# FFN of a four-layer model on one core: the high weight tile takes the operand's high and low parts in one 512-column matmul, and the two halves of the bank are added at eviction

## The reference

```python
def swiglu(h, w_gate, w_up, w_down):
    return (jax.nn.silu(h @ w_gate) * (h @ w_up)) @ w_down
# in each layer
h = h + mixer(rms_norm(h, mixer_g))
h = h + swiglu(rms_norm(h, ffn_g), w_gate, w_up, w_down)
```

## Time and profile before

| | us |
|---|---|
| median of three runs | 1203.58 (1201.99 to 1203.69) |
| the profiled execution's own time | 1202.35 |
| its span, first to last instruction | 1200.5 |
| PE busy | 1177.2, 98% of the span |
| DVE busy | 811.6, 68% |
| ACT busy | 589.2, 49% |
| mean DMA rate | 165 GB/s |

### The profile page before, as it was taken

One profiled execution on the slowest core, in us unless ns is written; L12 is line 12 of the kernel. 1 busy time (PEld: TensorE's weight loads), 2 busy tenths in 40 slices (PEclk: granted clock), 3 DMA queues, 4 the chain that ended last, 5 costly groups with the idle time before them and its releaser, 6 DMA issues.

```text
span 1200.5 us, 22339 instructions
## 1 busy us (share of the span) xinstructions
PE 1177.2 (98%) x9228; PEld 1142.8 (95%) x9228; DVE 811.6 (68%) x1302; ACT 589.2 (49%) x965; POOL 30.7 (3%) x54
## 2 busy tenths in 40 slices
PE   8999999999999799999999999999999899999999
PEld 8999999999998699999999999999998569999999
DVE  6867766655899577666656967666554897766642
ACT  6535444444745464445543545444444566544531
POOL 0120000000000000000000000000001200000000
PEclk8999999999999799999999999999999999999999
DMA  7543555555222045555543645555553323555551
GB/s 293 211 141 140 176 176 181 193 189 176 106 106 71 28 184 180 188 192 182 180 169 142 222 170 195 186 176 178 209 176 141 140 72 140 177 180 191 192 181 66
DMA packets 29046, 197.91 MB, mean 165 GB/s; under 512 B 3472, under 2 KB 4752, under 8 KB 5520
## 3 DMA queue, kind: packets, MB, share of 16 engines
q1 hardware_dynamic: 28656, 196.34, 45.7%
q10 hardware_dynamic: 288, 0.14, 0.0%
HBM read 195.41 MB, written 1.05 MB: 164 GB/s over the span
## 4 chain that ended last, share of the span: by engine, by line
PE 96%; DVE 2%; ACT 1%; DMA 0%; issue 0%; POOL 0%; DVEq 0%; ACTq 0%
PE banks L353 28%; PE banks L356 28%; PE banks L359 28%; PE banks L390 7%; PE banks L373 1%; PE banks L379 1%; PE banks L376 1%; DMA col<-cols 0%; PE banks L1276 0%; DVE scr L1493 0%; POOL scr L900 0%; DVE lo_t L284 0%; DVE scr L1476 0%; ACT scr L1337 0%; DVE scr L1481 0%
## 5 line engine op out<-in xcount | busy, mean ns | idle before, releaser
L353 PE MATMUL banks<-xh,hi_t 128*128 128x256 f32 x1856 | 530.0, 286 | 2.2 <-ACT hi_t L278 2.2
L359 PE MATMUL banks<-xh,lo_t 128*128 128x256 f32 x1856 | 526.3, 284 | 0.5 <-DVE lo_t L284 0.5
L356 PE MATMUL banks<-xl,hi_t 128*128 128x256 f32 x1856 | 526.3, 284 | 0.0
L284 DVE TENSOR_TENSOR lo_t<-raw_t,hi_t 128x1024 fp32r<-128x1024 f32 x368 | 444.8, 1221 | 12.2 <-ACT hi_t L278 7.7
L278 ACT ACTIVATE hi_t<-raw_t 128x1024 fp32r<-128x1024 f32 x368 | 380.6, 1048 | 71.2 <-PE banks L359 48.3
L353 PEld LDWEIGHTS banks<-xh,hi_t 128*128 128x128 f32 x1856 | 357.3, 192 | 3.0 <-ACT hi_t L278 2.4
L359 PEld LDWEIGHTS banks<-xh,lo_t 128*128 128x128 f32 x1856 | 357.3, 192 | 0.8 <-DVE lo_t L284 0.8
L356 PEld LDWEIGHTS banks<-xl,hi_t 128*128 128x128 f32 x1856 | 357.3, 193 | 0.6 <-issue 0.2
L353 PE MATMUL banks<-fh,hi_t 128*128 128x256 f32 x960 | 274.8, 286 | 4.8 <-ACT fh L1000 3.3
L356 PE MATMUL banks<-fl,hi_t 128*128 128x256 f32 x960 | 272.7, 284 | 0.5 <-DVE fl L840 0.4
L359 PE MATMUL banks<-fh,lo_t 128*128 128x256 f32 x960 | 272.3, 284 | 0.0
(11 more groups left out here) (160 smaller groups left out, 660.8 us busy)
## 6 DMA issues: line engine op xcount, KB each, us to landing
raw_t<-w SPq DMA_DIRECT2D x183, 1024.0 KB, 4.8
raw_t<-w SPq DMA_DIRECT2D x2, 512.0 KB, 7.0
out<-h SPq DMA_DIRECT2D x8, 128.0 KB, 3.7
cst<-consts SPq DMA_DIRECT2D x1, 800.0 KB, 11.1
h<-xT SPq DMA_DIRECT2D x1, 768.0 KB, 7.3
h<-xT SPq DMA_DIRECT2D x1, 256.0 KB, 4.2
pw<-poolw SPq DMA_DIRECT2D x1, 256.0 KB, 13.1
col<-cols SPq DMA_DIRECT2D x1, 193.0 KB, 8.1
```

The lines of the kernel that those rows point to most:

```text
L284: e.tensor_tensor(lo_t[:, p % RING, :], raw_of(p), hi_t[:, p % RING, :].bitcast(F32), ALU.subtract).then_inc(s_lo, 1)
L353: e.matmul(dst, hi_t[:, slot, c], hi[:, k, :], start=first, stop=False, skip_group_check=True)
L356: e.matmul(dst, hi_t[:, slot, c], lo[:, k, :], start=False, stop=False, skip_group_check=True)
L359: m = e.matmul(dst, lo_t[:, slot, c], hi[:, k, :], start=False, stop=last, skip_group_check=True)
```

## The change

The operand's two parts lie side by side in one tensor (`x2`, `f2`), so that they are 512 contiguous columns. In the FFN alone, `broad_tile` takes the place of `tile`: one matmul of 512 columns with the high weight tile fills a whole bank (high by high in columns 0 to 255, high by low in 256 to 511), and one of 256 columns with the low weight tile accumulates into the first half. Both parts of the operand are waited for before the first matmul. A block `u` now fills two banks, a pair of `PAIRS`, of which there are three; the RMS work of the FFNs moves to bank 2. At eviction ACT copies the second halves of the pair to SBUF (`side`), DVE adds the first halves to it (`add`, which frees the pair), and the scaling then reads and writes SBUF. On ACT the split that was due after the silu stands before it. For a row of the second product DVE adds the two halves to `h` one after the other, the second after the first is complete. The mixers keep `tile`.

```diff
-        xh = sb("xh", [P, KD, T], F32R)
-        xl = sb("xl", [P, KD, T], F32R)
-        fh = sb("fh", [P, KF, T], F32R)
-        fl = sb("fl", [P, KF, T], F32R)
+        x2 = sb("x2", [P, KD, 2, T], F32R)
+        f2 = sb("f2", [P, KF, 2, T], F32R)
+        xh, xl, fh, fl = x2[:, :, 0, :], x2[:, :, 1, :], f2[:, :, 0, :], f2[:, :, 1, :]
...
+        def broad_tile(e, g, bank, k, parts, first, last, arrives=None):
+            slot, r = piece(e, g)
+            c = slice(r * P, (r + 1) * P)
+            if r == 0:
+                e.wait_ge(s_hi, g // 8 + 1)
+            if arrives:
+                e.wait_ge(*arrives[0])
+                e.wait_ge(*arrives[1])
+            e.matmul(halves(banks[:, bank, :]), hi_t[:, slot, c], parts[:, k, :, :], start=first, stop=False,
+                     skip_group_check=True)
+            if r == 0:
+                e.wait_ge(s_lo, g // 8 + 1)
+            m = e.matmul(banks[:, bank, 0:T], lo_t[:, slot, c], parts[:, k, 0, :], start=False, stop=last,
+                         skip_group_check=True)
+            if g in MARKS:
+                m.then_inc(s_tiles, 1)
...
         def dve_ffn(e, f):
+            def add(u):
+                e.wait_ge(s_side, KF * f + u + 1)
+                e.tensor_tensor(halves(t_ring[u % 3]), pair_of(u, 0), halves(b_ring[u % 2]), ALU.add).then_inc(s_up, 1)
             lo_to(e, g0 + 32)
             dve_mean(e, i)
+            add(0)
             dve_dg(e, i)
+            add(1)
...
             for u in range(KF):
                 lo_to(e, c)
-                e.wait_ge(s_tiles, upto(g0 + 16 * max(u, 1) + 15))
-                e.tensor_tensor(halves(t_ring[u % 3]), halves(banks[:, UP_BANKS[u % 4], :]), ..., ALU.mult).then_inc(s_up, 1)
+                if u >= WIDE:
+                    add(u)
+                both = halves(t_ring[u % 3])
+                e.wait_ge(s_up, KF * f + u + 1)
+                e.tensor_tensor(both, both, stretch(rbc[:, :], 1, 2), ALU.mult).then_inc(s_scaled, 1)
...
-                e.tensor_tensor(h[:, n, :], banks[:, DOWN_BANKS[n % 3], 0:T], h[:, n, :], ALU.add).then_inc(s_h, 1)
+                m = dv.mark(e.tensor_tensor(h[:, n, :], ps[:, 0:T], h[:, n, :], ALU.add))
+                e.wait_ge(dv.sem, m)
+                e.tensor_tensor(h[:, n, :], ps[:, T:2 * T], h[:, n, :], ALU.add).then_inc(s_h, 1)
...
         def act_ffn(e, f):
+            def side(u):
+                e.wait_ge(s_tiles, upto(g0 + 16 * max(u, 1) + 15))
+                if u >= 2:
+                    e.wait_ge(s_up, KF * f + u - 1)
+                e.activation(halves(b_ring[u % 2]), pair_of(u, 1), ACT.Copy).then_inc(s_side, 1)
+            hi_to(e, g0 + 32)
+            side(0)
+            side(1)
             for u in range(KF):
                 hi_to(e, c)
-                e.wait_ge(s_up, KF * f + u + 1)
+                if u >= WIDE:
+                    side(u)
+                hi_to(e, c + 3)
+                e.wait_ge(s_scaled, KF * f + u + 1)
                 if u >= 2:
                     e.wait_ge(s_gated, KF * f + u - 1)
                 e.activation(s_ring[u % 2], t_ring[u % 3][:, 0:T], ACT.Silu).then_inc(s_silu, 1)
-                hi_to(e, c + 3)
```

More of the change, by code:

```diff
@@ L134 @@
 UP_BANKS = (0, 1, 6, 2)
[L135 removed]
+PAIRS = (0, 6, 4)
+DOWN_BANKS = (3, 7, 6)
 OUT_BANKS = (2, 3, 4, 5)
@@ L138, with rms_bank @@
 RMS_BANK = 7
+def rms_bank(i):
+    return 2 if i % 2 else RMS_BANK
 def att_banks():
@@ L343, in piece, with tile @@
             return p % RING, r
-        def tile(e, g, dst, k, hi, lo, first, last, arrives=None):
+        def tile(e, g, dst, k, parts, first, last, arrives=None):
             slot, r = piece(e, g)
@@ L352, in tile @@
                 e.wait_ge(*arrives[0])
-            e.matmul(dst, hi_t[:, slot, c], hi[:, k, :], start=first, stop=False, skip_group_check=True)
+            e.matmul(dst, hi_t[:, slot, c], parts[:, k, 0, :], start=first, stop=False, skip_group_check=True)
             if arrives:
                 e.wait_ge(*arrives[1])
-            e.matmul(dst, hi_t[:, slot, c], lo[:, k, :], start=False, stop=False, skip_group_check=True)
+            e.matmul(dst, hi_t[:, slot, c], parts[:, k, 1, :], start=False, stop=False, skip_group_check=True)
             if r == 0:
                 e.wait_ge(s_lo, g // 8 + 1)
-            m = e.matmul(dst, lo_t[:, slot, c], hi[:, k, :], start=False, stop=last, skip_group_check=True)
+            m = e.matmul(dst, lo_t[:, slot, c], parts[:, k, 0, :], start=False, stop=last, skip_group_check=True)
+            if g in MARKS:
[14 more added lines that the diff above has]
+                         skip_group_check=True)
             if g in MARKS:
@@ L401, in dve_mean @@
             e.wait_ge(s_col_sums, i + 1)
-            m = e.tensor_scalar(st[:, 0, :], banks[:, RMS_BANK, 0:2], 1.0 / D, EPS, ALU.mult, ALU.add)
+            m = e.tensor_scalar(st[:, 0, :], banks[:, rms_bank(i), 0:2], 1.0 / D, EPS, ALU.mult, ALU.add)
             if i == 4:
-                m = e.tensor_scalar(st[:, 2, :], banks[:, RMS_BANK, 2:4], 1.0 / D, None, ALU.mult)
+                m = e.tensor_scalar(st[:, 2, :], banks[:, rms_bank(i), 2:4], 1.0 / D, None, ALU.mult)
             m.then_inc(s_mean, 1)
@@ L419, in pe_spread @@
             e.wait_ge(s_dg, DG_AT[i] + n)
-            plain(e, banks[:, RMS_BANK, 0:n * P], one[:, :],
+            plain(e, banks[:, rms_bank(i), 0:n * P], one[:, :],
                   dg4[:, 0:n, :].rearrange("p a b -> p (a b)")).then_inc(s_spread, 1)
@@ L424, in dve_rbc @@
             e.wait_ge(s_spread, RBC_AT[i] + 1)
-            e.tensor_copy(rbc[:, :], banks[:, RMS_BANK, 0:T]).then_inc(s_rbc, 1)
+            e.tensor_copy(rbc[:, :], banks[:, rms_bank(i), 0:T]).then_inc(s_rbc, 1)
             e.wait_ge(s_rbc, RBC_AT[i] + 1)
-        s_up, s_silu, s_gated = sem("up"), sem("silu"), sem("gated")
+        s_side, s_up, s_scaled, s_silu, s_gated = sem("side"), sem("up"), sem("scaled"), sem("silu"), sem("gated")
         t_ring = [scratch(n * 512, 512) for n in range(3)]
@@ L433, in model_kernel, with pair_of @@
         m_ring = [scratch(2048 + n * T, T) for n in range(2)]
+        b_ring = [scratch(2560 + n * 512, 512) for n in range(2)]
+        def pair_of(u, half):
+            return banks[:, PAIRS[u % 3]:PAIRS[u % 3] + 2, half * T:(half + 1) * T]
         def pe_ffn(e, f):
@@ L439, in pe_ffn @@
                     for t in range(2):
-                        tile(e, g0 + 4 * k + 2 * v + t, banks[:, UP_BANKS[v], t * T:(t + 1) * T], k, xh, xl,
-                             k == 0 and t == 0, k == KD - 1, x_of(i, k) if v == 0 and t == 0 else None)
+                        broad_tile(e, g0 + 4 * k + 2 * v + t, PAIRS[v] + t, k, x2, k == 0, k == KD - 1,
+                                   x_of(i, k) if v == 0 and t == 0 else None)
             for u in range(WIDE, KF):
-                if u >= len(UP_BANKS):
-                    e.wait_ge(s_up, KF * f + u - len(UP_BANKS) + 1)
+                if u >= len(PAIRS):
+                    e.wait_ge(s_up, KF * f + u - len(PAIRS) + 1)
                 for t in range(2):
@@ L451, in pe_ffn @@
                             pe_spread(e, i)
-                        tile(e, g0 + c, banks[:, UP_BANKS[u % 4], t * T:(t + 1) * T], k, xh, xl, k == 0, k == KD - 1)
+                        broad_tile(e, g0 + c, PAIRS[u % 3] + t, k, x2, k == 0, k == KD - 1)
             for n in range(KD):
@@ L456, in pe_ffn @@
                 for k in range(KF):
-                    tile(e, g0 + UP_TILES + KF * n + k, banks[:, DOWN_BANKS[n % 3], 0:T], k, fh, fl, k == 0,
-                         k == KF - 1, f_of(s, k) if n == 0 else None)
+                    broad_tile(e, g0 + UP_TILES + KF * n + k, DOWN_BANKS[n % 3], k, f2, k == 0, k == KF - 1,
+                               f_of(s, k) if n == 0 else None)
         def dve_ffn(e, f):
@@ L540, in pe_out_block @@
             dst = banks[:, OUT_BANKS[j // 2], (j % 2) * T:(j % 2 + 1) * T]
-            tile(e, out_tile(g0, n_outer, j, n), dst, order[n], fh, fl, n == 0 and j % 2 == 0, n == KD - 1,
+            tile(e, out_tile(g0, n_outer, j, n), dst, order[n], f2, n == 0 and j % 2 == 0, n == KD - 1,
                  f_of(s, n) if j == 0 else None)
@@ L696, in pe_retention @@
                     for k in range(KD):
-                        tile(e, G_U + 16 * u + 8 * t + k, banks[:, u, t * T:(t + 1) * T], k, xh, xl, k == 0, k == KD - 1)
+                        tile(e, G_U + 16 * u + 8 * t + k, banks[:, u, t * T:(t + 1) * T], k, x2, k == 0, k == KD - 1)
             for u in range(2):
@@ L702, in pe_retention @@
                         c = 16 * u + 8 * t + k
-                        tile(e, G_G + c, banks[:, 2 + u, t * T:(t + 1) * T], k, xh, xl, k == 0, k == KD - 1)
+                        tile(e, G_G + c, banks[:, 2 + u, t * T:(t + 1) * T], k, x2, k == 0, k == KD - 1)
                         if c % 8 == 3:
```

11 lines of the change are left out of this document (5 added, 6 removed).

## The result

The changed kernel takes 1188.91 us (1188.36 to 1189.06, four runs) against 1203.55: ratio 0.988, interval 0.9863 to 0.9898. It is faster by 14.6 us where 27 were forecast.

What follows compares the result with a forecast made beforehand. PE's matmul pace in the FFNs (763.8 of 1200.5 us) was taken as the bound. -27.7 + 0.4 + 0.5 = -26.8 us on 1202.35 gave 1175.6, and half the run spread made 1176.2; range 1173.5 to 1182.

Steps and rivals of the forecast that it cites:

- PE's work: FFN tiles: two 256-column matmuls with high weights become one of 512, saving 13.1 ns in each of 2112 tiles, 27.7 us.
- the change of width costs nothing there: End of the V stage: going from 512-column to 256-column matmuls adds no time, so no term for it.
- The two-sided bounds of that term: A tile's high part takes between 213.3 ns (no fixed share left, 56 us saved) and 240 ns (nothing saved).
- The fixed share: Each float32r matmul on PE has 13.3 ns beyond its columns, and merging two saves one such share.
- the rival of a share of 3 ns: FFN tiles: merging saves only 3 ns per tile, 6.3 us, giving 1197 us; chance 0.03.
- the one of no gain: FFN tiles: merged matmul treated as two, tile stays at 360 ns, 1203 to 1204 us; chance 0.02.
- The eviction: Up phase: ACT's copy (0.60 us) and DVE's add (0.69) per block fit in PE's block of 5.55 us, costing nothing.
- The slower rival: Up phase: a split before ACT's copy makes the round 6.2 us and holds PE, about 1229 us; chance 0.05 with similar losses.
- The start of the down rows: Row 0, tile 21: low part ready at T + 7.1, needed at T + 7.28; 0.1 us stall per FFN, 0.4 allowed; stalls' chance 0.10.
- The end: End of the program: the output's store waits for the second addition, 0.46 us more, on the path for certain.

Runs made afterwards that it cites:

- a group of eight: Changed kernel with matmuls grouped by eight tiles, the 512-column ones first, then the 256-column ones: 1183.11 us, ratio 0.9841.
- the first two experiments: Changed kernel with the low tile also at 512 columns: 1400.9 us; changed kernel with the wide matmul cut in two of 256: 1203.12 us.
- the low-first kernel: Changed kernel with each tile's two matmuls exchanged, the low tile's 256-column one ahead of the 512-column one: 1176.83 us, ratio 0.9784.
- the scan: Changed kernel with one extra matmul before each of blocks 4 to 21: 24 of 54 blocks behind float32r ones at 346.7 to 347.1 ns per tile, 30 at 352.9 to 353.4.

## Why the prediction was wrong

**The step that failed** is the one on PE's work: "the change of width costs nothing there". It was read off one transition at the end of the V stage, a 512-column matmul followed by 256-column ones, and carried to a stream that alternates 2112 times. That direction is indeed free: its first two narrow steps are 113 and 119 ns. But the sentence "The trace before has no alternation of 512 and 256 columns beyond one" overlooks the other direction, which the trace before holds twice, at 35.71 and at 911.88, where a V stage begins behind 256-column matmuls:

```profile
35.59 0.28 PE L359 MATMUL banks<-xh,lo_t 128*128 128x256 f32 x1
35.71 0.40 PE L373 MATMUL banks<-hi_t,xh 128*128 128x512 f32 x1
35.94 0.40 PE L376 MATMUL banks<-hi_t,xl 128*128 128x512 f32 x1
36.17 0.39 PE L379 MATMUL banks<-lo_t,xh 128*128 128x512 f32 x1
36.40 0.40 PE L373 MATMUL banks<-hi_t,xh 128*128 128x512 f32 x1
36.64 0.39 PE L376 MATMUL banks<-hi_t,xl 128*128 128x512 f32 x1
36.87 0.39 PE L379 MATMUL banks<-lo_t,xh 128*128 128x512 f32 x1
```

Five wide steps from 35.71 to 36.87 take 1.16 us and not 5 x 226.7 = 1.13. In nanoseconds they are 233, 236, 229, 232 and 231: 28 too many, the same as at the head of a group of eight. They are also the "small irregularities" behind the 227.1 ns that the prediction reads off the whole stage: spread over 48 matmuls, 28 ns are 0.6 each. So the change of width had a visible price before, and the sum had no term for it.

Both widths have their pace of 226.7 and 120 ns when alone (the first two experiments). The alternation, in which every change comes before the last one has settled, has levels of its own. The lowest one, 346.7 ns, is exactly the sum that was forecast; the changed kernel sits at 353.3. The term was mis-sized thereby: 6.7 ns saved per tile in 516 of 528 tiles, and not 13.1. The price of a lone round, 20 ns per tile, would have foretold a loss; the runs alone could show that it would be 0 or 6.7. The two-sided bounds of that term, 213.3 and 240 ns for the tile's high part, did contain the 233.3 measured, but the range of the time was drawn from 226.7 to 227.1 alone. At the low level the forecast's sum is met: 1176.83 and 1177.44 us against 1176.2.

**The fixed share** was right. 13.3 ns belong to each matmul, and merging two saves them; the rival of a share of 3 ns (1197 us) and the one of no gain (1203) are both refuted by the FFN of 184.15 us. How much of the share arrives depends on the level: all 13.3 ns at 346.7, half at 353.3.

**The eviction** cost nothing, as forecast. ACT's copy takes 0.60 us (forecast 0.60), DVE's add 0.69, the handoff to the scaling 0.04. In the last block of the second FFN, against the earlier trace rows, down row 0 starting at 557.15:

```profile
557.35 0.60 ACT L555 ACTIVATE scr<-banks 128x512 f32<-128x512 f32 x1 [0.74 <-PE banks L383]
557.98 0.69 DVE L503 TENSOR_TENSOR scr<-banks,scr 128x512 f32<-128x512 f32 x1 [1.30 <-ACT scr L555]
558.71 0.69 DVE L519 TENSOR_TENSOR scr<-scr,rbc 128x512 f32<-128x512 f32 x1
562.26 0.42 DVE L495 TENSOR_TENSOR scr<-scr 128x256 f32<-128x256 f32 x1
562.59 1.22 DVE L290 TENSOR_TENSOR lo_t<-raw_t,hi_t 128x1024 fp32r<-128x1024 f32 x1
563.73 0.42 DVE L499 TENSOR_TENSOR f<-scr,f 128x256 fp32r<-128x256 f32 x1
```

The slower rival, a round of 6.2 us, didn't occur: PE waits for no release of a pair, and DVE still waits for the copy in 76 of the 88 blocks, 1.24 us on average.

**The start of the down rows** was judged right. (T before was 562.93 and not 562.97, which makes 0.04 us.) The last low part ends at 563.73 + 0.42 = 564.15, T + 7.00, where T + 7.1 was forecast. The tile that needs it comes at 564.57 here, T + 7.42; in the low-first kernel it comes at T + 7.28, and no tile of its row 0 takes more than 4 ns over 347. The 0.4 us allowed for it wasn't needed.

**The end** was right: the second addition starts 0.46 us after the first, and the store at 1184.61 and not 1184.15 (before, it came 0.45 us after the one addition).

```profile
1183.70 0.42 DVE L533 TENSOR_TENSOR h<-banks,h 128x256 f32<-128x256 f32 x1 [6.88 <-PE banks L383]
1184.16 0.42 DVE L535 TENSOR_TENSOR h<-banks,h 128x256 f32<-128x256 f32 x1
1184.61 0.33 SPq L266 DMA_DIRECT2D out<-h  x1
```

**What stays open** is what it is that repeats in TensorE or around it, and so has a phase against the alternation. The runs show the repetition (three tiles of 361, 349 and 350 ns at the high level) and that both widths must be present, but not its source, nor why a lone round costs 20 ns; nor can they foretell from an insertion's width which level will follow.

## What to carry to other kernels

Merging two matmuls that share a stationary tile saved the fixed share of one, 13.3 ns of float32r, where the new mixture of widths fell into its good phase, and half of it where it didn't. A forecast from the steps of each kind alone has to leave room in its range for a mixture that runs a few ns per instruction dearer, and the trace before has to be searched for changes of width in both directions: here one gave 8 ns back and the other cost 28. If PE is busy throughout and the starts don't repeat with the expected sum, exchange the order within the unit, or shift the stream by one small matmul: here the two reached 1176.83 and 1177.44 us against 1188.91. Neither is sure to help, as the scan shows; read the level behind it.

## What the hardware showed that was not expected

- An alternation of 512 and 256 columns ran at 346.7 or 353.3 ns per pair, with the same instructions, clock and data. The level stayed for up to 484 tiles and changed only at an interruption.
- One width alone has no such levels: 120 ns at 256 columns and 226.7 at 512, over whole FFNs, once the first five matmuls behind a change are past.
- A lone change from 256 to 512 columns cost 28 ns over five matmuls, one from 512 to 256 gave 8 ns back in two.
- A matmul of one column (two records of 112 ns) added to each FFN shortened it from 187.36 to 184.37 us, by 484 tiles x 6.67 ns = 3.2 us less its own time.
- The Trainium skill ("TensorE: Matmul & The Clock Gate", Back-to-back issue gap) gives the step of a matmul by itself as N/2.4 + 2.5 ns, one value for each width. By these runs the addition is 13.3 ns for float32r with a weight load for each matmul (120 ns at 256 columns, 226.7 at 512), and in a mixture of widths the step also depends on the phase.
